# The gate table of an expert layer written by indirect DMAs instead of one-hot products

## The reference

```python
q = (xi @ w_q).reshape(n, PEER_HEADS, 2, PEER_KEY_DIM)
s = jnp.einsum('nhpc,hpkc->nhpk', q, sub_keys).astype(jnp.float32)
ts, ti = lax.top_k(s, PEER_TOPK)
cand_s = (ts[:, :, 0, :, None] + ts[:, :, 1, None, :]).reshape(n, PEER_HEADS, PEER_TOPK * PEER_TOPK)
cand_i = (ti[:, :, 0, :, None] * PEER_NKEYS + ti[:, :, 1, None, :]).reshape(n, PEER_HEADS, PEER_TOPK * PEER_TOPK)
best_s, best_p = lax.top_k(cand_s, PEER_TOPK)
idx = jnp.take_along_axis(cand_i, best_p, axis=-1)
gate = jax.nn.softmax(best_s, axis=-1)
act = jax.nn.gelu(jnp.einsum('nd,nhkd->nhk', xi, u[idx]).astype(jnp.float32), approximate=False)
return jnp.einsum('nhk,nhkd->nd', (gate * act).astype(xi.dtype), v[idx])
```

## Time and profile before

| what | before |
|---|---|
| median of 3 runs | 2983.76 us (2981.37 to 2984.48) |
| the profiled execution, its own time | 2977.23 us |
| its span, first to last instruction | 2975.5 us |
| mean granted TensorE clock | 0.949 |
| TensorE, VectorE, ScalarE, GpSimd busy | 92%, 53%, 34%, 19% |
| HBM read and written | 366.98 MB and 67.11 MB |

### The profile page before, as it was taken

The page is one execution under the profiler, slowest core; times in us unless marked ns, Lnnn a source line. Parts: engine busy times, 40 slices in busy tenths (PEclk is TensorE's granted clock), DMA queues, the critical chain, the costliest instruction groups (busy, mean ns, idle before and its releaser), DMA issues. The chain is left out here.

```text
span 2975.5 us, 35996 instructions
## 1 busy us (share of the span) xinstructions
PE 2744.4 (92%) x13758; PEld 2341.7 (79%) x13758; DVE 1585.2 (53%) x3403; ACT 1000.4 (34%) x1499; POOL 571.4 (19%) x350
## 2 busy tenths in 40 slices
PE   7987677999999999999988898959999899899998
PEld 6865566888888888888988888956797678688886
DVE  1146334999566663223777777853585344433322
ACT  3114323333344443223323333342323652322222
POOL 3310020333200000004566666400132000000000
PEclk9978578999999999999999999979999999999999
DMA  4200024334444545446888888952232112333321
GB/s 145 75 6 6 1 86 135 115 119 142 137 168 169 202 181 219 149 156 202 292 301 319 302 311 318 364 205 79 64 86 85 42 44 92 107 92 99 93 99 64
DMA packets 281738, 436.65 MB, mean 147 GB/s; under 512 B 21408, under 2 KB 194496, under 8 KB 280544
## 3 DMA queue, kind: packets, MB, share of 16 engines
q1 hardware_dynamic: 259040, 367.17, 37.0%
q0 software_dynamic: 22528, 67.19, 6.3%
HBM read 366.98 MB, written 67.11 MB: 146 GB/s over the span
## 5 line engine op out<-in xcount | busy, mean ns | idle before, releaser
L1571 DVE TENSOR_TENSOR pe_wl<-pe_raw,pe_wh 128x1024 fp32r<-128x1024 f32 x272 | 353.2, 1300 | 346.2 <-ACT pe_wh L1414 334.2
L217 PE MATMUL bank<-pe_xh,pe_wh 128*128 128x512 f32 x1152 | 455.5, 395 | 9.9 <-DVE pe_wl L1571 9.9
L221 PE MATMUL bank<-pe_xh,pe_wl 128*128 128x512 f32 x1152 | 449.6, 390 | 0.0
L220 PE MATMUL bank<-pe_xl,pe_wh 128*128 128x512 f32 x1152 | 449.4, 390 | 0.0
L217 PE MATMUL bank<-pe_hh,pe_wh 128*128 128x384 f32 x1024 | 351.9, 344 | 46.1 <-DVE pe_wl L1571 38.1
L2279 DVE TENSOR_TENSOR s_wl<-s_raw,s_wh 128x1024 fp32r<-128x1024 f32 x143 | 198.7, 1393 | 308.0 <-ACT s_wh L2021 307.0
L220 PE MATMUL bank<-pe_hl,pe_wh 128*128 128x384 f32 x1024 | 349.7, 342 | 3.2 <-issue 3.2
L221 PE MATMUL bank<-pe_hh,pe_wl 128*128 128x384 f32 x1024 | 349.5, 341 | 0.4 <-issue 0.4
L1387 POOL DMA_INDIRECT pe_v_rows<-in_peer_v,pe_place_u x128 | 188.4, 1472 | 591.6 <-DMA scratch_gates<-pg_slices 399.9
L1414 ACT ACTIVATE pe_wh<-pe_raw 128x1024 fp32r<-128x1024 f32 x272 | 286.2, 1052 | 23.3 <-DMA p_gain<-in_ln_w 11.9
L217 PEld LDWEIGHTS bank<-pe_xh,pe_wh 128*128 128x128 f32 x1152 | 217.2, 189 | 52.9 <-issue 10.1
(11 more groups left out here) (436 smaller groups left out, 4990.9 us busy)
## 6 DMA issues: line engine op xcount, KB each, us to landing
pe_raw<-in_peer_u SPq DMA_DIRECT2D x128, 512.0 KB
pe_raw<-in_peer_v SPq DMA_DIRECT2D x128, 512.0 KB
scratch_hidden<-pe_a_out SPq DMA_DIRECT2D x128, 256.0 KB, 2.1
scratch_gates<-pg_slices SPq DMA_DIRECT2D x6, 4096.0 KB, 12.1
pe_gate<-scratch_gates SPq DMA_DIRECT2D x32, 768.0 KB
pe_a_in<-scratch_hidden SPq DMA_DIRECT2D x128, 192.0 KB
s_raw<-in_w_in SPq DMA_DIRECT2D x48, 512.0 KB, 3.8
s_raw<-in_w_gate_up SPq DMA_DIRECT2D x44, 512.0 KB, 3.9
```

Source lines behind the costliest of these rows:

```text
L217: first = pe.matmul(out, lhs[0], rhs[0], start=start, stop=False, skip_group_check=skip)
L220: pe.matmul(out, lhs[0], rhs[1], start=False, stop=False, skip_group_check=skip)
L221: return pe.matmul(out, lhs[1], rhs[0], start=False, stop=stop, skip_group_check=skip)
L1571: dve.tensor_tensor(wl[:, i % RING, :], raw[:, i % RAW, :], wh[:, i % RING, :].bitcast(F32), ALU.subtract).then_inc(S["w_lo"], 1)
```

## The change

The gate table is now a DRAM tensor of 128 x 128 x 384 (expert's first key, second key, token). SyncE clears it by 16 DMAs (`BLANKS`) of 8 planes each from a row of zeros, two in each three of its first loop turns. VectorE works out the place of each pick (`find_cells`) and, as a cell must hold the sum where a token picked an expert more than once, adds to each pick's gate the gates of earlier heads' picks of the same expert (`sum_repeats`). GpSimd writes the gates into the table (`set_gates`): for each head and each of three token tiles 16 indirect DMAs of 128 single words, 384 in all; head h's group waits for head h - 1's of the same tile, so that the last write holds the full sum. Two groups go between the pick batches, the rest after them. Then GpSimd raises `scattered`, for which SyncE waits before its first `load_hidden`. The one-hots, their products, copies and stores are gone, and so is the transfer of the first tile's picks (`own`). The gate is loaded per down item (192 KB) into four slots. VectorE multiplies the gate in ahead of its next split from the fourth item on. GpSimd fetches 16 elements first, then a row and an element in turn, and there are eight row slots; rows are no longer fetched before the activations are complete. Six of the sums of repeats (heads 0 and 1) and the places of batch 0 are made within batch 1, the others follow one per item from item 52.

The diff, cut to its core:

```diff
-FETCH, ROW_SLOTS = 8, 5
+FETCH, ROW_SLOTS = 8, 8
+BLANKS = 16
...
-        table = nc.dram_tensor("scratch_gates", (SLICES, P, PEER_KEYS, SLICE_TOKENS), F32, kind="Internal").ap()
+        table = nc.dram_tensor("scratch_gates", (PEER_KEYS, P, DENSE), F32, kind="Internal").ap()
+        cells = table.rearrange("n j (t one) -> (n j t) one", one=1)
...
             def load_hidden(n):
                 if n == 0:
-                    wait_slices(sp)
-                if n % QUAD == 0:
-                    q = n // QUAD
-                    if q >= 2:
-                        sp.wait_ge(S["gated"], QUAD * (q - 1))
-                    sp.dma_start(gate[:, q % 2, :, :, :].rearrange("p g k n -> p g (k n)"),
-                                 table[:, :, n:n + QUAD, :].rearrange("g j k n -> j g (k n)"))\
-                        .then_inc(gate_landed[q % 2], 16)
+                    sp.wait_ge(S["scattered"], 1)
...
                 sp.dma_start(a_in[:, n % 4, :], hidden[n, :, GATHERED:T]).then_inc(a_landed[n % 4], 16)
+                sp.dma_start(gate[:, n % 4, :], table[n, :, :]).then_inc(a_landed[n % 4], 16)
...
-                if i == TURN:
-                    sp.wait_ge(S["picked"], B)
-                    sp.wait_ge(S["hot_used"], B)
-                    sp.dma_start(own[:, :, :], pick[:, 0, :, :]).then_inc(S["own_landed"], 16)
-                k = i - SPREAD_FROM
-                if k > 0 and k * PER_STEP * SPREAD % SLICE_TOKENS == 0 and k <= SPREADS // PER_STEP:
-                    store_slice(k * PER_STEP * SPREAD // SLICE_TOKENS - 1)
+                if i % 3 < 2 and 2 * (i // 3) + i % 3 < BLANKS:
+                    k, n = 2 * (i // 3) + i % 3, PEER_KEYS // BLANKS
+                    sp.wait_ge(S["blank"], 1)
+                    sp.dma_start(table[k * n:(k + 1) * n, :, :].rearrange("n j t -> j n t"),
+                                 zeros[:, :].unsqueeze(1).to_broadcast([P, n, DENSE])).then_inc(S["zeroed"], 16)
...
+            def set_gates(h, t):
+
+                pool.wait_ge(S["cells_ready"], h * (NT - 1) + t)
+                if h:
+                    for r in range(K):
+                        pool.wait_ge(written[t - 1][r], 16 * h)
+                for r in range(K):
+                    at = h * K + r
+                    pool.indirect_dma_start(cells, bass.IndirectOffsetOnAxis(ap=cell_u[:, t, at:at + 1], axis=0),
+                                            value[:, t, at:at + 1], None).then_inc(written[t - 1][r], 16)
...
+                if b == 1:
+                    pool.wait_ge(S["zeroed"], 16 * BLANKS)
+                if 1 <= b < B - 1:
+                    set_gates(*next(groups))
...
-            pool.wait_ge(S["places_ready"], 1)
-            wait_slices(pool)
-            for r in range(ROW_SLOTS):
-                fetch_row(r)
+            for h, t in groups:
+                set_gates(h, t)
+            for t in range(1, NT):
+                for r in range(K):
+                    pool.wait_ge(written[t - 1][r], 16 * (HP // 2))
+            pool.sem_inc(S["scattered"], 1)
...
+            pool.wait_ge(S["places_ready"], B)
             for k in range(4):
                 pool.wait_ge(a_stored[k], 16 * NB // 4)
-            for c in range(PICKS // OWN_PART + 1):
-                for r in range(c * OWN_PART, min((c + 1) * OWN_PART, PICKS)):
...
-                for r in range(max((c - 1) * OWN_PART, ROW_SLOTS), c * OWN_PART):
-                    fetch_row(r)
+            for r in range(OWN_PART):
+                fetch_own(r)
+            for r in range(PICKS):
+                fetch_row(r)
+                if r + OWN_PART < PICKS:
+                    fetch_own(r + OWN_PART)
...
-                if i == TURN:
-                    turn_picks()
-                for g in spreads_after(i):
-                    spread(g)
-            pe.wait_ge(S["spread_taken"], SPREADS)
...
+                own, before = slice(h * K, (h + 1) * K), slice(0, h * K)
...
+                same, shape = work[:, 0:K * h * K].rearrange("p (r q) -> p r q", r=K), [P, K, h * K]
+                chain(dve.tensor_tensor(same, expert[:, t, own].unsqueeze(2).to_broadcast(shape),
+                                        expert[:, t, before].unsqueeze(1).to_broadcast(shape), ALU.is_equal))
+                chain(dve.tensor_tensor(same, same, pick[:, t, 2, before].unsqueeze(1).to_broadcast(shape), ALU.mult))
+                chain(dve.tensor_reduce(repeated[:, :], same, AX.X, ALU.add))
+                dve.tensor_tensor(value[:, t, own], pick[:, t, 2, own], repeated[:, :], ALU.add)\
+                    .then_inc(S["cells_ready"], 1)
...
-            for i in range(SPREAD_FROM - 2, N):
+            units = iter([(h, t) for h in range(2, HP // 2) for t in range(1, NT)])
+            for i in range(LAST_PICKS - 2, N):
+                n = i - DOWN + 3
+                if 4 <= n < NB:
+                    apply_gate(n)
                 if i + 2 < N:
                     split_lo()
-                for g in spreads_after(i + 1):
-                    one_hots(g)
-                n = i - DOWN + 3
+                for h, t in itertools.islice(units, 1):
+                    sum_repeats(h, t, hot[:, :, :, :, :].rearrange("p j g r k -> p (j g r k)"))
+                if 0 <= n < 4:
+                    apply_gate(n)
                 if 0 <= n < NB:
-                    apply_gate(n)
                     split_hidden(n)
```

More of the change, by code:

```diff
@@ L1211, in expert_stream, with place @@
     return first + second + third + [("down", n) for n in range(PEER_KEYS)]
+def place(nc, name, at, shape, dt=F32):
+    with ExitStack() as over:
+        if at:
+            over.enter_context(nc.sbuf_tensor(f"below_{name}", [P, at], F32))
+        return over.enter_context(nc.sbuf_tensor(name, shape, dt))
 def phase_peer(nc, bank, const, io, life):
@@ L1368, in _ @@
             chain = Chain(pool, S["gpsimd_steps"])
+            def set_gates(h, t):
[7 more added lines that the diff above has]
+                                            value[:, t, at:at + 1], None).then_inc(written[t - 1][r], 16)
+            groups = iter([(h, t) for h in range(HP // 2) for t in range(1, NT)])
+            pool.memset(zeros[:, :], 0.0).then_inc(S["blank"], 1)
             for b in range(B):
@@ L1601, in finish, with find_cells, sum_repeats @@
                 dve.wait_ge(S["picked"], b + 1)
+            def find_cells(b):
+                dve.wait_ge(S["hot_used"], b + 1)
+                part = slice(2 * b * K, 2 * (b + 1) * K)
+                chain(dve.scalar_tensor_tensor(expert[:, :, part], picks(b, 0), float(PEER_KEYS), picks(b, 1),
+                                               ALU.mult, ALU.add))
+                dve.tensor_scalar(cell_f[:, 0, part], expert[:, 0, part], float(T), lane[:, :], ALU.mult, ALU.add)
+                chain(dve.scalar_tensor_tensor(cell_f[:, 1:NT, part], expert[:, 1:NT, part], float(DENSE),
+                                               column[:, :].unsqueeze(2).to_broadcast([P, NT - 1, 2 * K]),
+                                               ALU.mult, ALU.add))
+                dve.tensor_copy(row_u[:, part], expert[:, 0, part])
+                dve.tensor_copy(cell_u[:, :, part], cell_f[:, :, part]).then_inc(S["places_ready"], 1)
+                dve.wait_ge(S["places_ready"], b + 1)
+            def sum_repeats(h, t, work):
+                own, before = slice(h * K, (h + 1) * K), slice(0, h * K)
+                if h == 0:
+                    dve.tensor_copy(value[:, t, own], pick[:, t, 2, own]).then_inc(S["cells_ready"], 1)
+                    return
+                same, shape = work[:, 0:K * h * K].rearrange("p (r q) -> p r q", r=K), [P, K, h * K]
[5 more added lines that the diff above has]
+                    .then_inc(S["cells_ready"], 1)
+                dve.wait_ge(S["cells_ready"], h * (NT - 1) + t)
             def pick_batch(b):
@@ L1618, in pick_batch @@
                     finish(b - 1)
+                if b == 1:
+                    find_cells(0)
+                    for h in range(2):
+                        for t in range(1, NT):
+                            sum_repeats(h, t, cand[:, :, :, :].rearrange("p g a b -> p (g a b)"))
                 chain(dve.tensor_copy(tsum[:, :], best[:, :, 0]))
@@ L1674, in weigh_own @@
                 part = slice(c * OWN_PART, (c + 1) * OWN_PART)
-                dve.tensor_tensor(h_own[:, part], a_own[:, part], own[:, 2, part], ALU.mult)\
+                dve.tensor_tensor(h_own[:, part], a_own[:, part], pick[:, 0, 2, part], ALU.mult)\
                     .then_inc(S["h_own_ready"], 1)
@@ L1800, in __init__ @@
             self.count[i] = counts[self.taker[i]]
-def place(nc, name, at, shape, dt=F32):
-    with ExitStack() as over:
-        if at:
-            over.enter_context(nc.sbuf_tensor(f"below_{name}", [P, at], F32))
-        return over.enter_context(nc.sbuf_tensor(name, shape, dt))
 def phase_second(nc, bank, io):
```

143 lines of the change are left out of this document (41 added, 102 removed).

## The result

The changed kernel takes 3217.68 us (median of 4 runs, 3212.83 to 3227.15), the kernel before beside it 2984.12 us: ratio 1.0787, 95% interval 1.0759 to 1.0815. I had forecast 2848 us. The profiled execution took 3212.83 us (span 3211.1) against a sum of 2841.

A forecast was written before the change was run, and what follows sets the result against it. TensorE's own instructions bound the up half; in the down half it waited for VectorE, held up by GpSimd's fetches. 2977 - 78 (up) - 58 (down) = 2841, plus 6.5 for the median: 2848 us, range 2822 to 2916.

The forecast's parts named there:

- The spread: Up items: 96 spreads on TensorE go, 87 us, and 12 transposes, 1.5 us; nothing covers them: -88.4 us.
- The clears: First 23 SyncE loop turns: 16 table clears, 4.5 us each, ahead of weight loads; taken as 0, up to 72 us.
- The sums of repeats: Last 18 VectorE units, one per up item, delay some weight splits: +5 us (bounds 0 and 9).
- The scatters: GpSimd in the up half: 1.39 us each beside splits, last at 1264 us, release at 1272: costs 5 us.
- a release up to 1267 is free: Change to the down items: TensorE loses nothing if the scatters are done and SyncE released by 1267 us.
- Rows and elements alternate: Down half: alternating fetches and eight slots remove VectorE's 10 us holes; 603.3 us becomes 545, -58 us.
- The gate load and order: Down half: gate loaded per item and multiplied ahead of the split; VectorE doesn't bind there, so 0.
- patch: Down half, 1400 to 1420 us: TensorE busy 15.81 of 20, clock 0.83; 7 us of it left in the 545.
- C: Rival, slower than before: single-word DRAM writes set GpSimd's issue pace; break-even 1.82 us per scatter, 3089 us at 2.1; chance 0.09.
- D: Rival: DMA engines at 315 GB/s bind the down half, no gain there: 2906 us; chance 0.07.
- E: Rival: the table clears starve the first items, 72 us at most: 2920 us; chance 0.03.
- B: Rival: scatters plainly late, 1.5 to 1.8 us each throughout; at 1.6, 2913 us; chance 0.17.

The follow-up runs named there:

- e2: Changed kernel without its 384 scatters and the waits for them; clears and sums of repeats stay: 2858.85 us, ratio to before 0.9614.
- e9: Changed kernel, every fourth scatter waiting for a VectorE split, first 16 element gathers of the down half held to two per item: 2835.21 us, ratio 0.9559.
- e4: Kernel before with only the alternation of rows and elements and eight row slots added: 2917.86 us, ratio 0.9818.
- e7: Changed kernel with a one-column GpSimd memset before every scatter, first 16 element gathers held to two per item: 3174.69 us, ratio 1.0693.
- e5: Changed kernel with 64 offsets per scatter instead of 128, same count and order: 3225.96 us, ratio 1.0857.
- e18: The kernel of e9 run again, on one chip with e19: 2833.92 us, ratio 0.9553.
- e19: The kernel of e9 without the hold on the first 16 element gathers, on one chip with e18: 2833.92 us, ratio 0.9557.

## Why the prediction was wrong

By its own steps, with the traces of the groups where the steps can be seen apart:

1. **The spread, -88.4 us: right.** e2's last up item was taken at 1279.4 us; 1362.9 - 88.4 + 5 was 1279.5. (These two terms are seen only together.)
2. **The clears, 0: right.** From 460 to 620 us TensorE was busy 149.89 us, before 150.13, beside DMA engines at 0.83 instead of 0.40. A clear landed in 7.9 us instead of the 4.5 of the sum, under the same cover.
3. **The sums of repeats, +5: right.** TensorE waited 4.5 us in four places for the splits (e2 and e9, 600 to 1283 us).
4. **The scatters: right on GpSimd, wrong for the kernel.** I had 1.39 us each and the last at 1264; e9 had 1.36 per scatter once the sums were done, 1.40 over all of the run, and its last at 1257.1; the changed kernel had its last at 1264.5. The collision with VectorE's split is there (1.34 us instead of 0.96, one scatter of four). By the reason given in the Trainium skill (SBUF — State Buffer, Who interferes with whom), which is called inferred there, a tensor_tensor would have had none with descriptor generation; these rows speak against it as the earlier trace rows did. The step that failed is the silent one before the sum: that GpSimd's issue costs only GpSimd's time. The prediction prices the release of `scattered` and nothing else ("a release up to 1267 is free"). TensorE, put down as undisturbed at 5.43 us per item beside a busy GpSimd, lost 349 us. The same section of the Trainium skill says, in its practical consequences, that a DMA never contends with a compute engine; the row 860 to 900 us above, 8 matmuls in 40 us at a DMA share of 0.02, and e2, in which that loss is gone with the scatters, say that issuing a long run of them can hold one up, by a way that stays open.
5. **Rows and elements alternate, -58 us: right for the length of the down half.** 544.1 us in e4 against 545 (the whole kernel gained 51 us in its group); in the changed kernel 480 of 480 us busy from 1700 to 2180 us at 347 GB/s. Most of its 21 us too many are the stall of the first gathers (44.71 of 60 us busy from 1640 to 1700), of which I had left 7 us in: with these held, e7's down half was 17 us shorter than e5's.
6. **The gate load and order, 0:** nothing in the down half speaks against it.

Without the stall the sum holds: 2834 us in a group without it (e18, e19: the changed kernel with a wait that holds nothing up, e18 also with the first gathers held), against a kernel before of 2966; that is 132 us, where the forecast had 136 (2984 to 2848).

Of the rivals, C gave the right sign for another reason: it wanted GpSimd itself to be slow, 1.82 us a scatter or more, and GpSimd ran at 1.27 in the median, 1.43 on average. D, E and B don't show. None of them had one engine's issue slow another's. The clue was in the profile: the earlier trace rows show TensorE busy 15.81 of 20 us at clock 0.83 from 1400 to 1420 us. In that trace GpSimd issued 32 gathers in a row from 1366.3 us on, and TensorE's gaps without a wait began at the 25th, at 1400.3 us. I took 7 us of this "patch" over into the sum without asking what it was. It looks like the same stall (that it is the same isn't shown), and the change was about to issue 352 DMAs in a row.

**Open:** what of TensorE is held up, and its hand-over to ScalarE with it; why the stall sets in after 12 to 24 close DMAs and outlasts them by more than 10 us; why TensorE also woke at 900.89 us, for eight matmuls, with GpSimd issuing at its usual pace; what differs between the groups; whether plain DMAs of GpSimd do it in a group that stalls.

## What to carry to other kernels

A long run of GpSimd's indirect DMAs isn't hidden because GpSimd is idle and the DMA engines are free: put the run's length, not only its end, among the costs, and look at TensorE's row beside any such run of the kernel before. Tie the run to the progress of the engine that mustn't suffer, or leave 0.6 us between two DMAs. Four scatters to an item were 1 to 2% faster than the kernel before in the groups that stall, where the free run was 8% slower; in the groups that don't stall e9, e18 and e19 were 4% faster, but there their waits held nothing up. TensorE with gaps "<- issue" inside an item, at a DMA share near zero, is the sign. And a kernel that lives near such an edge has to be timed on several chips and at several times: 2834 and 2947 us for one program here.

## What the runs showed of the hardware

- A scatter of 128 words takes GpSimd as long as a gather (962 and 944 ns, then 0.30 us), one of 64 words 892 ns, a plain DMA of 128 words 537 ns.
- An operation of GpSimd of 0.12 us fits into the 0.30 us between two indirect DMAs and delays nothing (e7).
- In a stall TensorE makes a matmul every 0.65 to 1.43 us at first and every 2.1 to 3.5 us later, stands still for up to 21 us between two items, and the granted clock falls to 0.50, that is 1.2 GHz.
- The stall goes on after GpSimd's last DMA: 6 matmuls from 930 to 944 us, with no other engine busy.
